# Routing of a two-block network: unscaled transposes, scale on the routing product, experts chosen by logits, weights behind the gathered rows

## The reference

```python
def rmsnorm(x, g):
    xf = x.astype(jnp.float32)
    inv = lax.rsqrt(jnp.mean(xf * xf, axis=-1, keepdims=True) + RMS_EPS)
    return (xf * inv * g.astype(jnp.float32)).astype(x.dtype)
...
    h2 = rmsnorm(x, ffn_norm[l]).reshape(b * s, d)
    y = hierarchical_moe(h2, ...)
    x = x + y.reshape(b, s, d)
return rmsnorm(x, final_norm)
...
def hierarchical_moe(t, w_group, b_group, w_inner, b_inner, w_gate, w_up, w_down):
    group_p = jax.nn.softmax((t @ w_group + b_group).astype(jnp.float32), axis=-1)
    g_w, g_idx = lax.top_k(group_p, 1)
    inner_all = jnp.einsum('nd,gde->nge', t, w_inner) + b_inner
    inner_logits = jnp.take_along_axis(inner_all, g_idx[:, :, None], axis=1)[:, 0]
    inner_p = jax.nn.softmax(inner_logits.astype(jnp.float32), axis=-1)
    e_w, e_idx = lax.top_k(inner_p, TOP_K_INNER)
    e_w = e_w / jnp.sum(e_w, axis=-1, keepdims=True)
    # combine = g_w * one_hot(g_idx) * sum of one_hot(e_idx) * e_w
    # y = sum over experts of silu(t w_gate) * (t w_up) * combine, times w_down
```

## Time and profile before

| | us |
|---|---|
| median of 3 runs (lowest, highest) | 1556.15 (1555.81, 1556.73) |
| profiled execution | 1554.53 |
| its span, first to last instruction | 1552.6 |
| PE busy | 1387.1 (89%) |
| DVE busy | 680.1 (44%) |
| ACT busy | 528.5 (34%) |
| mean granted TensorE clock, of 1 | 0.928 |

### The profile page before, as it was taken

The page is one execution under the profiler, slowest core; times in us unless marked ns, Lnnn a source line. Parts: engine busy times, 40 slices in busy tenths (PEclk is TensorE's granted clock), DMA queues, the critical chain, the costliest instruction groups (busy, mean ns, idle before and its releaser), DMA issues. The chain is left out here.

```text
span 1552.6 us, 19336 instructions
## 1 busy us (share of the span) xinstructions
PE 1387.1 (89%) x7886; PEld 1050.7 (68%) x7886; DVE 680.1 (44%) x1321; ACT 528.5 (34%) x854; POOL 43.5 (3%) x36
## 2 busy tenths in 40 slices
PE   6999896778999999998989779999698868999996
PEld 3887574555678888877867559998485446666663
DVE  3222536774132433558445854556516333222122
ACT  2225332343442322415544447444226221111112
POOL 0000000210000000002000110000000000000000
PEclk9999998798699999998999988999798878999998
DMA  9422121114320424224422003455132644999990
GB/s 386 169 102 82 54 81 55 55 55 169 130 81 27 163 89 156 109 81 144 140 105 81 28 1 108 164 191 190 43 136 81 267 180 184 410 405 409 410 401 32
DMA packets 34222, 238.96 MB, mean 154 GB/s; under 512 B 4304, under 2 KB 4432, under 8 KB 6224
## 3 DMA queue, kind: packets, MB, share of 16 engines
q1 hardware_dynamic: 34128, 237.66, 40.1%
HBM read 236.59 MB, written 1.05 MB: 153 GB/s over the span
## 5 line engine op out<-in xcount | busy, mean ns | idle before, releaser
L226 DVE TENSOR_TENSOR pieces_lo<-weight_ring,pieces_hi 128x1024 fp32r<-128x1024 f32 x154 | 186.9, 1223 | 311.2 <-ACT pieces_hi L218 311.2
L244 PE MATMUL proj<-h_hi,pieces_hi 128*128 128x512 f32 (+1 forms) x816 | 288.7, 354 | 7.3 <-DVE pieces_lo L226 3.7
L246 PE MATMUL proj<-h_hi,pieces_lo 128*128 128x512 f32 (+1 forms) x816 | 284.7, 349 | 0.0
L245 PE MATMUL proj<-h_lo,pieces_hi 128*128 128x512 f32 (+1 forms) x816 | 283.2, 347 | 0.0
L218 ACT ACTIVATE pieces_hi<-weight_ring 128x1024 fp32r<-128x1024 f32 x158 | 165.4, 1053 | 237.7 <-PE score L246 149.9
L244 PEld LDWEIGHTS proj<-h_hi,pieces_hi 128*128 128x128 f32 x816 | 156.3, 191 | 36.2 <-issue 14.7
L245 PEld LDWEIGHTS proj<-h_lo,pieces_hi 128*128 128x128 f32 x816 | 156.3, 191 | 22.8 <-issue 1.7
L246 PEld LDWEIGHTS proj<-h_hi,pieces_lo 128*128 128x128 f32 x816 | 155.9, 191 | 20.0
L1854 PE MATMUL turn<-expert_parts,e_gathered 128*64 128x256 f32 x768 | 85.3, 379 | 0.0
L1854 PEld LDWEIGHTS turn<-expert_parts,e_gathered 128*64 128x64 f32 x768 | 55.1, 137 | 32.3 <-issue 6.3
L733 PE MATMUL turn<-l_diag,l_probs 128*128 128x128 f32 x320 | 46.9, 301 | 32.7 <-DVE l_diag L1151 15.7
(11 more groups left out here) (410 smaller groups left out, 2121.1 us busy)
## 6 DMA issues: line engine op xcount, KB each, us to landing
weight_ring<-in_stream SPq DMA_DIRECT2D x110, 1024.0 KB, 5.1
expert_parts<-in_experts SPq DMA_DIRECT2D x70, 1024.0 KB, 10.8
weight_ring<-in_experts SPq DMA_DIRECT2D x26, 1024.0 KB, 10.9
l_rows<-in_rows SPq DMA_DIRECT2D x2, 768.0 KB, 15.6
l_y_attn<-in_ada_first SPq DMA_DIRECT2D x1, 1024.0 KB, 5.4
l_y_gla<-in_ada_first SPq DMA_DIRECT2D x1, 1024.0 KB, 7.5
l_y_sgu<-in_ada_first SPq DMA_DIRECT2D x1, 1024.0 KB, 8.4
l_q<-in_ada_first SPq DMA_DIRECT2D x1, 1024.0 KB, 10.2
```

Of the source, the lines that this page charges most:

```text
L226: eng.tensor_tensor(self.part(self.lo_ring[:, n % NPIECE, :], kind), self.raw(slot, c, kind), self.part(self.hi_ring[:, n % NPIECE, :], ki ...
L244: pe.matmul(out, sh, mh, start=start, stop=False)
L245: pe.matmul(out, sh, ml, start=False, stop=False)
L246: return pe.matmul(out, sl, mh, start=False, stop=stop)
```

## The change

The list begins with the transposes, which read x_latent as it is. The squares of both tiles follow each other on ACT, with one root and one reciprocal for both, whose completion is `scaled`. The scaled rows are no longer written: XH is a copy of x_latent with the scale as ACT's factor, XL one instruction on DVE that scales and subtracts. `rows` stands ahead of `route`. The routing product is scaled as DVE adds the bias. Groups and experts are chosen by the largest logits; the second by adding −1e30 to the first. The exponentials and the combine weights are a step of their own, `weights`, behind the gathers of pair 0; `gw` 0, which needs them, stands behind `gu` 0 and waits for the new signal `combined`. A routing product waits for the transposes it reads and no longer for all.

```diff
-    s = [("sel", first // 4)] + [("gather", (first // 2, b)) for b in range(4)] + [("gw", first // 4)]
+    s = [("sel", first // 4)] + [("gather", (first // 2, b)) for b in range(4)]
+    s += [("weights", 0)] if first == 0 else [("gw", first // 4)]
     for n in range(first, end):
         q = n // 2 + 1 if 2 * (n // 2 + 1) < end else None
         s += [("gu", n)]
+        if n == 0:
+            s += [("gw", 0)]
...
-        main_work = [("norm", 0), ("norm", 1)] + [("turnx", i) for i in range(4)]
-        main_work += [("route", 0), ("route", 1), ("rows", 0), ("rows", 1), ("rank", 0)] + MAIN_STEPS
+        main_work = [("turnx", i) for i in range(4)] + [("norm", 0), ("norm", 1)]
+        main_work += [("rows", 0), ("rows", 1), ("route", 0), ("route", 1), ("rank", 0)] + MAIN_STEPS
...
-                        last = pe.transpose(acc[:, n * P:(n + 1) * P], XS[:, t, k * P:(k + 1) * P], ident)
+                        last = pe.transpose(acc[:, n * P:(n + 1) * P], xlat[:, t, k * P:(k + 1) * P], ident)
...
-                        pe.wait_ge(*PT.evacuated(J("turnx", 2)))
-                        pe.wait_ge(*PT.evacuated(J("turnx", 3)))
                     acc = PT.open(pe, J("route", i))
                     for k in range(KT):
+                        if i == 0 and k % 2 == 0:
+                            pe.wait_ge(*PT.evacuated(J("turnx", k // 2)))
...
+                        pe.wait_ge(*sig.combined.at(1))
...
-                    act.activation(st[:, 4 + i:5 + i], st[:, i:i + 1], ACT.Sqrt, bias=eps).then_inc(*sig.norm_root.one())
-                elif kind == "route":
-                    act.wait_ge(*sig.route_max.at(i + 1))
-                    act.activation(GP[:, i, :], L[:, i, 0:G], ACT.Exp, bias=MX[:, i, 0:1], accum_out=MX[:, i, 1:2])\
-                        .then_inc(*sig.route_exp.one())
-                elif kind == "rank":
+                    if i == 1:
+                        act.activation(st[:, 4:6], st[:, 0:2], ACT.Sqrt, bias=eps).then_inc(*sig.norm_root.one())
+                elif kind == "weights":
                     act.wait_ge(*sig.inner_max.at(1))
+                    for t in range(2):
+                        act.activation(GP[:, t, :], L[:, t, 0:G], ACT.Exp, bias=MX[:, t, 0:1], accum_out=MX[:, t, 1:2])
                     for t in range(2):
                         last = act.activation(IP[:, t, :], IL[:, t, :], ACT.Exp, bias=MX[:, t, 2:3], accum_out=MX[:, t, 3:4])
                     last.then_inc(*sig.inner_exp.one())
                 elif kind == "rows":
-                    act.wait_ge(*sig.scaled.at(i + 1))
-                    act.activation(XH[:, i, :], XS[:, i, :], ACT.Copy).then_inc(*sig.rows_hi.one())
+                    act.wait_ge(*sig.scaled.at(1))
+                    act.activation(XH[:, i, :], xlat[:, i, :], ACT.Copy, scale=st[:, 4 + i:5 + i]).then_inc(*sig.rows_hi.one())
...
-                    dve.wait_ge(*sig.norm_root.at(i + 1))
-                    link(dve.reciprocal(st[:, 4 + i:5 + i], st[:, 4 + i:5 + i]))
-                    dve.tensor_scalar(XS[:, i, :], xlat[:, i, :], st[:, 4 + i:5 + i], None, ALU.mult)\
-                        .then_inc(*sig.scaled.one())
+                    if i == 1:
+                        dve.wait_ge(*sig.norm_root.at(1))
+                        dve.reciprocal(st[:, 4:6], st[:, 4:6]).then_inc(*sig.scaled.one())
...
-                    dve.tensor_tensor(L[:, i, :], PT.tile(J("route", i))[:, 0:36], par[:, M_BR:M_BR + 36], ALU.add)\
-                        .then_inc(*PT.evac(J("route", i)))
-                    dve.wait_ge(*PT.evacuated(J("route", i)))
-                    link(dve.reduce_max(MX[:, i, 0:1], L[:, i, 0:G], AX.X))
-                    dve.tensor_scalar(MX[:, i, 0:1], MX[:, i, 0:1], -1.0, None, ALU.mult).then_inc(*sig.route_max.one())
+                    if i == 0:
+                        dve.wait_ge(*sig.scaled.at(1))
+                    link(dve.scalar_tensor_tensor(L[:, i, :], PT.tile(J("route", i))[:, 0:36], st[:, 4 + i:5 + i],
+                                                  par[:, M_BR:M_BR + 36], ALU.mult, ALU.add))
+                    dve.engine_nop().then_inc(*PT.evac(J("route", i)))
                 elif kind == "rank":
 
-                    dve.wait_ge(*sig.route_exp.at(2))
-                    link(dve.reciprocal(MX[:, :, 4:5], MX[:, :, 1:2]))
-                    link(dve.tensor_tensor(GP[:], GP[:], MX[:, :, 4:5].to_broadcast([P, 2, G]), ALU.mult))
-                    link(first_max(dve, link, GP[:], G1[:], G2[:], OH[:], MX, 5, G))
+                    link(first_max(dve, link, L[:, :, 0:G], G1[:], G2[:], OH[:], MX, 5, G))
...
-                    link(dve.tensor_reduce(MX[:, :, 6:7], IL[:], AX.X, ALU.max))
-                    dve.tensor_scalar(MX[:, :, 2:3], MX[:, :, 6:7], -1.0, None, ALU.mult).then_inc(*sig.inner_max.one())
-                    dve.wait_ge(*sig.inner_exp.at(1))
-                    link(dve.reciprocal(MX[:, :, 7:8], MX[:, :, 3:4]))
-                    link(dve.tensor_tensor(IP[:], IP[:], MX[:, :, 7:8].to_broadcast([P, 2, E]), ALU.mult))
-
-                    link(first_max(dve, link, IP[:], I1[:], I2[:], O1[:], MX, 8, E))
-                    link(dve.scalar_tensor_tensor(I1[:], O1[:], -2.0, IP[:], ALU.mult, ALU.add))
+                    link(first_max(dve, link, IL[:], I1[:], I2[:], O1[:], MX, 8, E))
+                    link(dve.scalar_tensor_tensor(I1[:], O1[:], -1e30, IL[:], ALU.mult, ALU.add))
                     link(first_max(dve, link, I1[:], IP[:], I2[:], O2[:], MX, 9, E))
...
-                    link(dve.tensor_tensor(MX[:, :, 10:11], MX[:, :, 8:9], MX[:, :, 9:10], ALU.add))
-                    link(dve.reciprocal(MX[:, :, 11:12], MX[:, :, 10:11]))
...
+                elif kind == "weights":
+
+                    dve.tensor_scalar(MX[:, :, 0:1], MX[:, :, 5:6], -1.0, None, ALU.mult)
+                    dve.tensor_scalar(MX[:, :, 2:3], MX[:, :, 8:9], -1.0, None, ALU.mult).then_inc(*sig.inner_max.one())
+                    dve.wait_ge(*sig.inner_exp.at(1))
+                    dve.tensor_reduce(MX[:, :, 5:6], GP[:], AX.X, ALU.max)
+                    dve.reciprocal(MX[:, :, 4:5], MX[:, :, 1:2])
...
+                    dve.tensor_tensor(I1[:], IP[:], O1[:], ALU.mult)
+                    link(dve.tensor_tensor(I2[:], IP[:], O2[:], ALU.mult))
...
+                    last.then_inc(*sig.combined.one())
                 elif kind == "rows":
                     dve.wait_ge(*sig.rows_hi.at(i + 1))
-                    dve.tensor_tensor(XL[:, i, :], XS[:, i, :], XH[:, i, :].bitcast(F32), ALU.subtract).then_inc(*sig.rows_lo.one())
+                    dve.scalar_tensor_tensor(XL[:, i, :], xlat[:, i, :], st[:, 4 + i:5 + i], XH[:, i, :].bitcast(F32),
+                                             ALU.mult, ALU.subtract).then_inc(*sig.rows_lo.one())
```

More of the change, by code:

```diff
@@ L306, in __init__ @@
         self.one_hot = signal("one_hot")
+        self.combined = signal("combined")
         self.selected = signal("selected")
@@ L1790, in tensor_steps @@
                 if kind == "turnx":
-                    if i == 0:
-                        pe.wait_ge(*sig.scaled.at(2))
                     acc = PT.open(pe, J("turnx", i))
@@ L1994, in vector_steps @@
                     last.then_inc(*sig.one_hot.one())
-                    link(dve.tensor_tensor(MX[:, :, 10:11], MX[:, :, 8:9], MX[:, :, 9:10], ALU.add))
-                    link(dve.reciprocal(MX[:, :, 11:12], MX[:, :, 10:11]))
-                    link(dve.tensor_tensor(MX[:, :, 8:10], MX[:, :, 8:10], MX[:, :, 11:12].to_broadcast([P, 2, 2]), ALU.mult))
-                    link(dve.tensor_tensor(O1[:], O1[:], MX[:, :, 8:9].to_broadcast([P, 2, E]), ALU.mult))
-                    link(dve.tensor_tensor(O2[:], O2[:], MX[:, :, 9:10].to_broadcast([P, 2, E]), ALU.mult))
-                    link(dve.tensor_tensor(O1[:], O1[:], O2[:], ALU.add))
-                    link(dve.tensor_tensor(O1[:], O1[:], MX[:, :, 5:6].to_broadcast([P, 2, E]), ALU.mult))
-                    for t in range(2):
-                        last = dve.tensor_tensor(COMB[:, t], O1[:, t, :].unsqueeze(1).to_broadcast([P, G, E]),
-                                                 OH[:, t, :].unsqueeze(2).to_broadcast([P, G, E]), ALU.mult)
-                    link(last)
                     dve.wait_ge(*PT.ready(J("rank")))
@@ L2095, in _ @@
             for t in range(2):
[L2096 removed]
+                dve.wait_ge(*sig.norm_root.at(t + 2))
                 link(dve.reciprocal(st[:, 6 + t:7 + t], st[:, 6 + t:7 + t]))
```

19 lines of the change are left out of this document (16 added, 3 removed).

## The result

| | us |
|---|---|
| this, median of 4 runs | 1535.88 (1525.89, 1529.33, 1542.44, 1544.41) |
| before, median of 4 runs beside them | 1555.98 (1545.01, 1555.81, 1556.15, 1556.73) |
| ratio of the two, 95% interval | 0.9877 (0.9841 to 0.9912) |
| this, profiled execution (span) | 1542.44 (1540.7) |

The profiled execution is one of the upper pair. That it took 1542.4 to the tenth, the figure forecast for the median, is luck: for this execution the forecast was 1540.8; the block saved 0.9 us more than that, and the work ahead of the block, which the change doesn't touch, took 2.7 us more.

The account below looks back on a forecast made before the run. One ACT, DVE and PE routing chain ahead of the PE-bound expert stage was taken as the bound: −14.66 to the first gather, +0.94 for an exposed evacuation, −13.7 us in all, forecasting 1542.4 us, range 1539.2 to 1546.0.

Parts of the forecast that it names:

- First gather: End of the routing chain: first gathering matmul 17.39 us behind ACT's first square instead of 32.05, saving 14.66 us.
- The scaling copy: High half of the scaled rows, multiplying by a scale in memory: 0.10 us more, taken between bounds 0 and 0.25.
- Fourth evacuation: Behind the gathers, ahead of gate and up 0: PE waits 0.94 us that the combine products used to hide.
- PE's branch: Transposes and routing products at full clock: done by 1263.5, 1.2 us before DVE gets to the logits.
- The weights: Combine-weight step behind the gathers: 5.6 us from the fourth evacuation, covered by 7.1 us of gate and up 0.
- The four gathers stay 6.67 us: Gathering matmuls on PE keep their old length, 1288.81 to 1295.48, since they begin after a rest in both orders.
- rival 2: PE runs faster in rank and gathers: 1538.2 us if none is slow, or 1 to 2 us gained; chance 0.12.
- One sign of being wrong: First gate and up matmul to the end changes by more than the 1.8 us of combine products moved there.
- rival 1: Transposes and routing products run at 0.50 clock, second logits late: +2.7 us, time 1545.1; chance 0.15.
- rival 3: The expert weight stream sets the end, so an earlier start buys nothing: 1556 us; chance 0.03.
- rival 4: Clock stays at 0.50 into the expert stage after PE's stop ahead of gate and up 0: 1557.8 us; chance 0.03.
- The step that failed: Sum's end: profiled execution, forecast at 1540.8 us, lay 1.6 below the median of the runs, giving 1542.4.

Follow-up runs that it names:

- e7: Changed kernel with the inner choice's exponentials and division put back, results unused: one run, 1541.77 us; first gather 18.77 us behind the first square, 17.24 without the edit.
- e3: Changed kernel with the transposes waiting again for the scale: one run, 1543.08 us; first gather 21.55 us behind the first square, 17.24 without the edit.
- e4: Changed kernel with the combine products ahead of gate and up 0 again, weights still behind the gathers: one run, 1551.62 us; first square to end 288.58 us.
- e1: Changed kernel unedited, twelve runs beside the kernel before: five from 1526.64 to 1531.82 us, seven from 1538.81 to 1544.46; ratio 0.9925.
- e5: Changed kernel plus 16 unneeded 128x512 products on PE ahead of line 810's first product in layer 0: six runs, median 1532.66 us.
- e6: Kernel before the change plus 16 unneeded 128x512 products ahead of line 810 in layer 0: twelve runs, median 1545.47 us, ratio to before 0.9954.
- e9: Changed kernel plus 16 dense products, second low half behind the one-hot rows, and 24 plus 8 small products: median 1526.81 us, ratio to before 0.9827.
- e10: Changed kernel with the 16 dense products alone, run once more: six runs, median 1529.90 us, ratio to before 0.9853.
- e12: Changed kernel plus 24 and 8 unneeded small PE products behind routing and rank products: one run, 1540.15 us; first square to end −2.93 us.
- e2: Changed kernel with the second low half behind the one-hot rows and 24 plus 8 small PE products: twelve runs, median 1537.72 us, ratio 0.9908.

## Why the prediction was right about the change and wrong about the time

**The chain was right, term by term** (behind the first square; forecast, then measured). Start of the transposes 0.04, 0.02. Scale ready 4.16, 4.17. First low half 5.33, 5.35. Logits 7.93, 7.75: the two low halves took 2.40 from start to start of the next and not 2.60. Choice 8.43, 8.34. Rank products 12.95, 12.86. First gather 17.39, 17.24. The scaling copy costs 0.10 more than the plain one (2.19 against 1.99 for two), the value taken; it was a choice between bounds, and it happened to be right. Fourth evacuation 0.94 forecast, 0.83 of wait measured. PE's branch over 6.74 behind the square, 6.63 measured. The weights took 4.3 us (1283.15 to 1287.47; 5.6 forecast), under 7.13 of gate and up. e7, e3 and e4 priced the removed round trip, the early transposes and the new place of `gw` one at a time.

**One term of the sum was off.** "The four gathers stay 6.67 us": they took 5.84 (1276.66 to the last one's end at 1282.50), since the clock came up inside them. That is the near half of rival 2, for which I had 1 to 2 us; it gave 0.83. With the evacuation the distance to gate and up 0 is 0.94 us under the forecast (6.67 for 7.61); the gather is 0.15 early, and the end 0.25 late (2.02 for 1.77). The three make the gap between −13.7 and −14.56. One sign of being wrong was passed by this: from gate and up 0 to the end 2.02 us more, where 1.8 was the limit; 1.79 of it is on PE. Of rival 1 nothing happened (stretches of 1.00 to 1264), of rival 3 nothing (no wait on a part; 1.00 and 241.15 of 245 us busy), and rival 4's fall of the clock at gate and up 0 did not occur.

**The step that failed** is the last one of the sum: "It lay 1.6 below the median of the runs, 1556.15: 1542.4 us". It takes the kernel's time ahead of `experts` for one value, known to 1 us, and puts into the range only what the routing may do. The runs fall into two groups, 13 to 15 us apart, in both kernels (e1), while the block itself takes the same in both (281.28 and 280.97). The three runs shown of before, within 0.9 us, all fell in the upper one. The four runs of after split two and two, so their median, 1535.88, lies in a gap where no run of this kernel did. The cause was in my own rows: the 30.72 us at 0.50 with a busy PE. I read it as evidence of what the clock might do elsewhere and did not ask whether it does so each time. e5, e6, e9 and e10 show that the upper group hangs on it: with the dense products ahead of it no upper group was left in 29 runs. Half of that stretch, 15.4 us, below 1542.4 is 1527: a range that took it in would have reached that far down. That is the most it can give, an estimate from the earlier trace rows; between the two profiles the stretch itself made 7.6 us.

**Rules and measurements.** The two low halves take 2.48 us together. The Trainium skill (Vector Engine (DVE) Microarchitecture Reference, section 7) has this operation at half throughput with two fp32 sources in SBUF. Read against 1.22 us, that would have made an estimate of 2.44 each; it does not hold for this form. PE rests 1.04 and 0.35 us around the transposes, and they run at 1.00; in the routing the clock was low behind rests of 5 to 6 us: e3, e4, the rank products. The rule that small rests between groups of matmuls let it fall and rise (the Trainium skill, TensorE: Matmul & The Clock Gate, section "A second HAM failure mode: psum-queue depth-cycling"; the prediction names the section ahead of it) was not borne out here: the small rests cost no clock. Nor does a rest explain the stretch of the earlier trace rows, in which PE was busy throughout.

**Open.** Why the clock comes back near 410 us in one execution and not in another, with PE's instructions the same up to there, no run settles. The stretch parts the two profiles by 7.6 us (0.22 at its first product, 7.85 at the fourth turn of L820); at the first square it is 10.39. The other 2.5 us comes in later pieces, which no experiment took apart, and no trace shows the rest of the 13 to 15 us between the groups: e1's profile is of the slowest of its five. Whether the −16.9 in the lower groups differs from the −14.7 in the upper, few runs leave open.

## What to carry to other kernels

Before a time is forecast, ask of every stretch of the profile at half clock whether it must be there in each execution: a few equal runs do not show a second value, and a forecast can't be narrower than that. A chain over three engines can be re-added from rows of one trace to 0.2 us; what is uncertain is the clock behind it. Where PE rests 6 us ahead of dense work, cheap matmuls whose results nobody reads can pay for themselves: 2.9 us in e12.

## What the runs showed of the hardware

- PE busy without a break got half clock for 30.72 us, over fp32 products of 128 and 64 rows by 128 columns (L810, L813, 0.79 for two against 0.48 at full clock). Sixteen products of 512 columns in 3.92 us ahead of them were followed by 1.00 through the same work, in all four profiles with them (e5, e6, e9, e10).
- Behind a rest of 5.07 us (e4) the clock read 0.52 over the next 7 us, though PE worked 6.61 of them: expert products too can start at half speed.
- 32 extra products of 128 columns in the routing (24 and 8, `ident` by `ident`) held 1.00 over the 21 us from the first square in e12, e2 and e9. In e12 they cost the chain nothing; in e2 the rank products started 0.2 us late behind them.
